# Linear attention's levels one slot later, the widest copied by ScalarE, other banks for its outputs, and own regions for the last feed-forward's inputs

## The chip, the cores and the metric

One core of a Trainium2 chip runs the whole program. The metric is the device time of one execution in microseconds; of the kernel before there are three runs. Four engines compute: TensorE (PE; matmuls and, as PEld, its weight loads), VectorE (DVE), ScalarE (ACT) and GpSimd (POOL). SyncE (SP) issues the weight transfers. They run side by side and wait for each other through semaphores.

## The reference, cut to what matters

```python
# h: [512 tokens, 1024 features], float32; three mixer layers, four feed-forwards
h = h + 0.5 * swiglu_ffn(rmsnorm(h))                   # ffn0
h = h + mixer1(rmsnorm(h)) @ w_mix_out                 # short convolution and gated delta rule
h = rmsnorm(h + 0.5 * swiglu_ffn(rmsnorm(h)))          # ffn1
# second block, layer 0: gated linear attention, 4 heads, beside attention on a memory of 256 rows
q, k, v, g, lr, mq = split(rmsnorm(h) @ gla_w_in)
b = cumsum(log_sigmoid(lr @ w_gate_up + b_gate) / 16)
A[i, j] = sum_d q[i, d] * k[j, d] * exp(b[i, d] - b[j, d])      # for i >= j
o = rmsnorm(A @ v) * silu(g)
h = h + concat(o, mem_attention(mq, mem)) @ w_out[0]
h = h + conv_ffn(rmsnorm(h))                           # ffn2
# layer 1: sparse attention (compressed, selected, windowed), beside memory attention
h = h + concat(nsa(rmsnorm(h)), mem_attention(mq, mem)) @ w_out[1]     # nsa_out
h = h + conv_ffn(rmsnorm(h))                           # ffn3
out = rmsnorm(h)
```

## The kernel before, in words

**Stages.** The program is a chain of dense stages, each a list of weight panels (128 x up to 1024) and output tiles (`Dense`, `Plan`). For a float32 result each operand is the sum of a high and a low part: ScalarE rounds the panel to `wH` (L407), VectorE subtracts to get `wL` (L445), and TensorE makes three matmuls, `wH`·`xH`, `wH`·`xL`, `wL`·`xH` (L589 to L591; with tokens as rows L583 to L585). There are four panel slots in `raw` and two in `wH`, `wL`: a panel is split one ahead of its use, once the panel two before it is used up. The order of work on each engine is written out by hand at the end of the program, one list for each engine: `after` on TensorE, `extra` and `ahead` on VectorE and `extra` on ScalarE hang other work behind or ahead of one tile of a dense stage.

**Linear attention.** `A` is not formed through one decay, but block by block in levels. The level of width w takes late queries and early keys of each block of 2w, both scaled by exponentials of gate sums relative to the block's middle. For a level, VectorE makes two differences of the gate sums (`level_sub_dve`, L2171, L2172), ScalarE their exponential (L2196), VectorE the products with queries and keys (`level_mul_dve`, L2214, L2215), TensorE the block products into banks 4 to 7 (`level_pe`), and VectorE copies them to `A256`, `A128` and `AD` (`take_dve`: L2232 for width 256, L2237 for 128, L2241 for 64, L2252 for narrower ones). There are widths 256 to 1, levels 0 to 8, and the diagonal blocks, level 9, which come first (L2290, copied at L2262). On TensorE the diagonal level runs ahead of stage gla_v, the wide one (level 0, L2300) behind its tile 1, the next ones behind tiles 3, 5, 7, 9 and 11 and behind tiles 0, 1 and 3 of gla_g. gla_v has 12 tiles of 256 columns in banks 0 to 3 in turn, copied by ScalarE (L1931); gla_g has 6 of 512, copied by VectorE in two pieces (L789, `evac_packed`). The memory attention's result stays in banks 2 and 3 until VectorE has made `m_lo` of it (L2063); tile 2 of gla_v waits for that. Then come eight outputs (`go_pe`: L2389, L2391, L2394), in banks 0 to 3 in turn, each copied by VectorE (L2417), squared by ScalarE (L2367) and summed by TensorE (L2401, `go_norm_pe`, from the fourth output on).

**The last feed-forward.** nsa_out writes 8 tiles, in two rounds of a loop of four, with `xH`, `xL` as inputs. VectorE adds each to `hT` (L827). ffn3_up reads `xH`, `xL` again, now filled from `hT`: ScalarE writes `xH` (`x_hi`, L845) once all matmuls of nsa_out are done (`refill_act`), VectorE `xL` (`x_lo`, L850), ScalarE squares (L860) for the norm, which GpSimd adds up (L907). ffn3_up's first tile takes the inputs one by one as they come. `g_hi`, `g_lo` hold the feed-forward's inner values for the second matmul.

```python
def bank_free_pe(pe, n, g):
    if n == 0 and g < 2:
        pe.wait_ge(sem("a_out"), g + 1)
...
def go_pe(pe, t):
    if t == 0:
        pe.wait_ge(sem("a_out"), a_before(len(LEVEL_ORDER)))
        wait_all(pe, stage_end("gla_g") + stage_end("gla_v"))
...
    o = bank[t % 4][0:96]
```

Of the kernel before, what the change touches and what calls it, by code (L numbers as in the profile page):

```python
# [5 lines left out]
ALU = mybir.AluOpType  # L6
# [128 lines left out]
def build(nc, A, out):  # L135

    with ExitStack() as ctx:
# [35 lines left out]
        g_hi_f = g_hi[:].bitcast(F32)  # L173
        w_hi3 = nc.alloc_sbuf_tensor_at("w_hi3", [P, SLOT], F32R, offset=at_arena + 4 * 10 * R)
# [30 lines left out]

        def up_stage(k, w, f):

            return Dense(f"ffn{k}_up", NF // 2, [[panel(w, KD, c + P * u, P, 2 * P)] for c in (0, FF) for u in range(2)],
                         [features(b, b, P, 0) for b in range(4)], (xH, xL), xfill(f))

        def down_stage(k, w):
# [4 lines left out]
            return Dense(f"ffn{k}_down", 1, panels, tiles, (g_hi, g_lo), None, by_rows=True)  # L216
# [478 lines left out]
        def g_split_act(act, k, f):  # L695
# [66 lines left out]
        def down_pe(pe, k):  # L762

            s = plan.stages[f"ffn{k}_down"]
            for f in range(NF):
# [3 lines left out]
                gh, gl = g_hi[:, f % 4, :], g_lo[:, f % 4, :]  # L769
# [1372 lines left out]
        A_COUNT = [2, NH, 2] + [1] * 7  # L2142

# [81 lines left out]
        def take_dve(dve, pos):  # L2225
# [3 lines left out]
            if n == 0:  # L2229
                for h in range(NH):  # L2230
                    dve.wait_ge(sem("a_sum"), base + h + 1)
                    nc.vector.tensor_copy(A256[:, h], bank[4 + h][:].rearrange("p (k s) -> p k s", k=2))\  # L2232
                      .then_inc(sem("a_out"), 1)
            elif n == 1:
# [30 lines left out]

        def bank_free_pe(pe, n, g):
# [1126 lines left out]
```

## Time and profile before

| | |
|---|---|
| median of 3 runs | 2419.6 us (2419.26 to 2421.55) |
| profiled execution | 2420.1 us, its span 2417.7 us |
| TensorE busy | 2360.8 us, 98% |
| VectorE busy | 1333.9 us, 55% |
| ScalarE busy | 921.3 us, 38% |
| GpSimd busy | 156.1 us, 6% |
| mean granted TensorE clock | 0.99 |
| linear attention, gla_v's first matmul to the first output | 1150.3 to 1251.5 us |
| ffn3_up's first matmul | 2040.0 us |

### The profile page before, as it was taken

The page shows a single profiled execution, that of the slowest core. Times are in us where ns is not written, and L with a number is a line of the kernel's source. Part 1 is how long each engine was busy: PE and PEld are TensorE (multiplying, and loading weights), DVE is VectorE, ACT ScalarE, POOL GpSimd, SP SyncE. Part 2 cuts the span into 40 slices and gives each one's busy share as a digit, 9 for nine tenths or more (in the row PEclk, how much of TensorE's full clock was granted, in tenths as well). Part 3 has the DMA queues.
Part 4 walks back from the last instruction along what each step waited for, and adds up shares of the span by engine and source line. Part 5 has one row for each costly group of instructions (what it writes and reads, how often), then busy time and mean ns, then how long its engine had stood idle before and what let it go on. Part 6 is the DMA issues. An engine that isn't in the chain of part 4 may idle for free.

```text
span 2417.7 us, 31976 instructions
## 1 busy us (share of the span) xinstructions
PE 2360.8 (98%) x12187; PEld 1927.1 (80%) x12187; DVE 1333.9 (55%) x2039; ACT 921.3 (38%) x1440; POOL 156.1 (6%) x151
## 2 busy tenths in 40 slices
PE   8999999999999999999999999999999989999999
PEld 7888887678778888877877888888887667888887
DVE  4444337667454444346867766644436874666633
ACT  4222225633442223244434333423224873433323
POOL 3000001024020000030001000000010001000001
PEclk9999999999999999999999999999999999999999
DMA  5333223220233332232213333232843102333322
GB/s 152 91 99 96 97 88 86 71 70 19 70 88 94 96 95 95 98 97 62 68 47 96 88 97 101 87 97 86 187 135 107 47 17 86 97 96 95 96 96 78
DMA packets 319650, 215.80 MB, mean 89 GB/s; under 512 B 49306, under 2 KB 302765, under 8 KB 319545
## 3 DMA queue, kind: packets, MB, share of 16 engines
q1 hardware_dynamic: 316280, 200.40, 28.8%
q0 software_dynamic: 3264, 13.94, 1.8%
q8 instruction: 73, 1.20, 0.2%
q14 instruction: 33, 0.26, 0.0%
HBM read 212.17 MB, written 8.44 MB: 91 GB/s over the span
## 4 chain that ended last, share of the span: by engine, by line
PE 88%; DVE 8%; ACT 2%; issue 1%; DMA 0%; POOL 0%; SPq 0%; POOLq 0%; DVEq 0%; ACTq 0%
PE bank L589 18%; PE bank L591 17%; PE bank L590 17%; PE bank L776 6%; PE bank L778 6%; PE bank L777 6%; PE bank L966 2%; DVE arena L2867 1%; PE bank L2815 1%; DVE wL L445 1%; DVE arena L2906 1%; PE bank L1716 1%; DVE xL L850 1%; PE bank L583 1%; PE bank L1822 1%
## 5 line engine op out<-in xcount | busy, mean ns | idle before, releaser
L589 PE MATMUL bank<-xH,wH 128*128 128x512 f32 x1920 | 761.8, 397 | 7.2 <-DVE xL L850 5.2
L591 PE MATMUL bank<-xH,wL 128*128 128x512 f32 x1920 | 750.8, 391 | 0.0
L590 PE MATMUL bank<-xL,wH 128*128 128x512 f32 x1920 | 750.6, 391 | 0.0
L445 DVE TENSOR_TENSOR wL<-raw,wH 128x1024 fp32r<-128x1024 f32 (+1 forms) x357 | 445.5, 1248 | 516.5 <-ACT wH L407 516.1
L407 ACT ACTIVATE wH<-raw 128x1024 fp32r<-128x1024 f32 (+1 forms) x357 | 374.9, 1050 | 758.4 <-PE bank L591 355.5
L589 PEld LDWEIGHTS bank<-xH,wH 128*128 128x128 f32 x1920 | 361.2, 188 | 95.5 <-issue 20.2
L590 PEld LDWEIGHTS bank<-xL,wH 128*128 128x128 f32 x1920 | 361.1, 188 | 79.1 <-issue 3.9
L591 PEld LDWEIGHTS bank<-xH,wL 128*128 128x128 f32 x1920 | 360.9, 188 | 78.3 <-issue 0.8
L776 PE MATMUL bank<-g_hi,wH 128*128 128x512 f32 x704 | 274.2, 390 | 1.5 <-DVE wL L445 1.5
L777 PE MATMUL bank<-g_lo,wH 128*128 128x512 f32 x704 | 273.9, 389 | 0.0
L778 PE MATMUL bank<-g_hi,wL 128*128 128x512 f32 x704 | 273.9, 389 | 0.0
L2481 ACT ACTIVATE arena<-arena,par 128x512 f32<-128x512 f32 x88 | 63.5, 723 | 271.9 <-DVE arena L2513 271.9
L776 PEld LDWEIGHTS bank<-g_hi,wH 128*128 128x128 f32 x704 | 132.2, 188 | 29.9 <-DVE wL L445 2.8
L778 PEld LDWEIGHTS bank<-g_hi,wL 128*128 128x128 f32 x704 | 132.2, 188 | 27.6
L777 PEld LDWEIGHTS bank<-g_lo,wH 128*128 128x128 f32 x704 | 132.2, 188 | 27.4
L2513 DVE TENSOR_TENSOR arena<-bank,rstd 128x512 f32<-128x512 f32 x88 | 60.6, 690 | 82.2 <-PE bank L591 82.1
L803 ACT ACTIVATE arena<-arena 128x512 f32<-128x512 f32 x44 | 27.6, 631 | 176.8 <-DVE arena L810 176.8
L907 POOL TENSOR_TENSOR rstd<-sq 128x512 f32<-128x512 f32 x7 | 9.7, 1384 | 1264.7 <-ACT sq L860 1264.7
L966 PEld LDWEIGHTS bank<-ident,arena 128*128 128x128 f32 (+4 forms) x467 | 54.5, 147 | 45.6 <-issue 23.1
L966 PE MATMUL bank<-ident,arena 128*128 128x128 f32 (+4 forms) x467 | 71.7, 295 | 18.6 <-DVE arena L2906 8.8
L812 DVE TENSOR_TENSOR arena<-bank,rstd 128x512 f32 (+1 forms) x44 | 30.4, 691 | 107.4 <-PE bank L591 107.4
L810 DVE TENSOR_TENSOR arena<-bank,rstd 128x512 f32<-128x512 f32 x44 | 30.2, 691 | 82.1 <-PE bank L591 82.0
(347 smaller groups left out, 2601.8 us busy)
## 6 DMA issues: line engine op xcount, KB each, us to landing
raw<-in_ffn_w_in SPq DMA_DIRECT2D x88, 512.0 KB, 3.8
raw<-in_w_up SPq DMA_DIRECT2D x88, 512.0 KB, 3.8
raw<-in_ffn_w_out SPq DMA_DIRECT2D x44, 512.0 KB, 3.5
raw<-in_w_down SPq DMA_DIRECT2D x44, 512.0 KB, 3.5
raw<-in_w_mix_in SPq DMA_DIRECT2D x28, 512.0 KB, 3.9
raw<-in_w_kv_shared SPq DMA_DIRECT2D x12, 512.0 KB, 6.3
rel_wide<-rel_rows POOLq DMA_DIRECT2D x12, 512.0 KB, 11.6
arena<-rel_wide POOLq DMA_DIRECT2D x12, 448.0 KB, 4.2
```

What stands on the lines that cost most here:

```text
L407: nc.scalar.activation(hi[:, 0:n], raw[:, k, 0:n], ACT.Copy).then_inc(sem("w_hi"), 1)
L445: nc.vector.tensor_tensor(lo[:, 0:n], raw[:, k, 0:n], hi[:, 0:n].bitcast(F32), ALU.subtract)\
L589: pe.matmul(o, wh, xa, start=a, stop=False)
L590: pe.matmul(o, wh, xb, start=False, stop=False)
L591: last = pe.matmul(o, wl, xa, start=False, stop=z)
L776: pe.matmul(bank[m][:], wh, gh, start=f == 0, stop=False)
L777: pe.matmul(bank[m][:], wh, gl, start=False, stop=False)
L778: last = pe.matmul(bank[m][:], wl, gh, start=False, stop=f == NF - 1)
L812: nc.vector.tensor_tensor(g[:, bass.ds(2 * i + t - 2, 1), :], one(bank[t][:]), one(rstd[:]), ALU.mult)\
L966: return pe.transpose(o, i, ident[0:k, 0:k])
L2481: nc.scalar.activation(cv[:, t, :], us[:, t, :], ACT.Copy, scale=conv_columns(s, i, t)[2])\
L2513: nc.vector.tensor_tensor(us[:, t, :], bank[t][:], rstd[:], ALU.mult).then_inc(sem("evac_dve"), 1)
```

## The change

- Levels: the diagonal level moves on TensorE from ahead of gla_v to behind its tile 1, levels 0 to 4 from behind tiles 1, 3, 5, 7, 9 to behind 3, 5, 7, 9, 11, level 5 from behind tile 11 to behind tile 0 of gla_g, levels 6 and 7 from behind tiles 0 and 1 to behind 1 and 2. Level 8 stays behind tile 3.
- VectorE's and ScalarE's lists are reordered to suit. The second pair of scans (`gate_scan_dve`) stands behind a split instead of ahead of it, `m_lo` ahead of the diagonal copies.
- Level 0's four banks are copied by ScalarE (`far_act`), with a semaphore of their own; `taken` counts the others.
- Output t goes to bank (t + 2) mod 4 and, for the first four, waits for that bank's own copy of gla_g instead of for all.
- nsa_out becomes one round of eight tiles. ffn3_up's inputs get regions of their own (`xH4`, `xL4`), so that `x_hi`, `square` and `x_lo` of tile j - 1 stand beside tile j of nsa_out. ffn3_down's inner values take the freed `xH`, `xL`.
- One activation of one column at the start is dropped.

```diff
+        xH4 = nc.alloc_sbuf_tensor_at("xH4", [P, KD, S], F32R, offset=at_arena + 4 * 10 * R)
+        xL4 = nc.alloc_sbuf_tensor_at("xL4", [P, KD, S], F32R, offset=at_arena + 4 * 12 * R)
...
+        def x_home(f):
+
+            return (xH4, xL4, xH4f) if f == 10 else (xH, xL, xHf)
+
+        def g_home(k):
+
+            return (xH[:, 0:4], xL[:, 0:4], xHf[:, 0:4]) if k == 3 else (g_hi, g_lo, g_hi_f)
...
-            return Dense(name, 2, [[panel(w, KD, P * j, P, 4 * P)] for j in range(4)],
-                         [features(b, b, P, 0) for b in range(4)], (xH, xL), xfill(f))
+            return Dense(name, 1, [[panel(w, KD, P * j, P)] for j in range(KD)],
+                         [features(j % 4, j, P, 0) for j in range(KD)], (xH, xL), xfill(f))
...
-                        pe.wait_ge(sem("go"), 5 + m)
+                        pe.wait_ge(sem("go"), 5 + (m + 2) % 4)
...
-            nc.scalar.activation(gain4[:, 0:1], eps[:], ACT.Copy).then_inc(sem("warm"), 1)
...
+        TAKEN = [2, 0, 2] + [1] * 7
...
+        def far_act(act):
+
+            for h in range(NH):
+                act.wait_ge(sem("a_sum"), a_before(1) + h + 1)
+                nc.scalar.activation(A256[:, h], bank[4 + h][:].rearrange("p (k s) -> p k s", k=2), ACT.Copy)\
+                  .then_inc(sem("far_out"), 1)
...
             elif n == 1:
-                pe.wait_ge(sem("a_out"), a_before(1) + g + 1)
+                pe.wait_ge(sem("far_out"), g + 1)
             elif n in (2, 3):
-                pe.wait_ge(sem("a_out"), a_before(1) + n + 1)
+                pe.wait_ge(sem("far_out"), n + 1)
...
             if t == 0:
-                pe.wait_ge(sem("a_out"), a_before(len(LEVEL_ORDER)))
-                wait_all(pe, stage_end("gla_g") + stage_end("gla_v"))
-            if t >= 4:
+                pe.wait_ge(sem("far_out"), NH)
+                pe.wait_ge(sem("a_out"), taken(len(LEVEL_ORDER)))
+                wait_all(pe, stage_end("gla_v"))
+            if t < 4:
+                pe.wait_ge(sem("evac_dve"), plan.evac(plan.stages["gla_g"], 0, t + 2))
+            else:
                 pe.wait_ge(sem("go"), t - 3)
...
-            dense_act(act, "nsa_out", nothing)
-            refill_act(act, 10, 7, "nsa_out", "ffn3_up")
+            ready = h_from("nsa_out")
+
+            def next_operand(k):
+                x_hi(act, 10, k, ready(k))
+                square(act, 7, k, ready(k))
+            dense_act(act, "nsa_out", nothing, extra={(0, j): lambda j=j: next_operand(j - 1) for j in range(1, KD)})
+            x_hi(act, 10, KD - 1, ready(KD - 1))
+            split_second(act, "ffn3_up")
+            square(act, 7, KD - 1, ready(KD - 1))
...
-            dense_dve(dve, "nsa_out", residual(1.0))
-            for k in range(KD):
-                x_lo(dve, 10, k)
+            dense_dve(dve, "nsa_out", residual(1.0), ahead={(0, j): lambda j=j: x_lo(dve, 10, j - 1) for j in range(1, KD)})
+            x_lo(dve, 10, KD - 1)
...
-            level_pe(pe, 0)
             dense_pe(pe, "gla_v", after={0: lambda: mem_round_pe(pe, 0, 5),
-                                         1: lambda: (level_pe(pe, 1), pe.wait_ge(sem("x_ready"), xbase(5) + 2)),
-                                         **{2 * n + 1: lambda n=n: level_pe(pe, n + 1) for n in range(1, 6)}})
-            dense_pe(pe, "gla_g", after={0: lambda: level_pe(pe, 7), 1: lambda: level_pe(pe, 8), 3: lambda: level_pe(pe, 9)})
+                                         1: lambda: (level_pe(pe, 0), pe.wait_ge(sem("x_ready"), xbase(5) + 2)),
+                                         **{2 * n + 3: lambda n=n: level_pe(pe, n + 1) for n in range(5)}})
+            dense_pe(pe, "gla_g", after={t: lambda t=t: level_pe(pe, t + 6) for t in range(4)})
```

What the reordering does to the queues is seen best in the instructions themselves. VectorE at the start of gla_v: `wL` is a split; L2119 are the scans; L2171, L2172 the differences, L2214, L2215 the products of a level; L2262 the diagonal copies, L2063 `m_lo`, L2232 the copies of the wide level. Before:

```order
L445 TENSOR_TENSOR wL<-raw,wH 128x1024
L2171 TENSOR_TENSOR arena<-arena 96x8x128
L2172 TENSOR_TENSOR arena<-arena 96x8x128
L2214 TENSOR_TENSOR arena<-arena 96x4x256
L2215 TENSOR_TENSOR arena<-arena 96x4x256
L2171 TENSOR_TENSOR arena<-arena 96x16x64
L2172 TENSOR_TENSOR arena<-arena 96x16x64
L2262 COPY_PREDICATED arena<-ident,bank 64x8x64 x4
L2063 TENSOR_TENSOR m_lo<-bank,m_hi 128x512 x2
L2214 TENSOR_TENSOR arena<-arena 96x8x128
L2215 TENSOR_TENSOR arena<-arena 96x8x128
L2232 COPY arena<-bank 128x512 x4
```

In the changed kernel the same operations have other line numbers (L456 the split, L2131 the scans, L2188, L2189 the differences, L2231, L2232 the products, L2075 `m_lo`, L2274 the diagonal copies):

```order
L456 TENSOR_TENSOR wL<-raw,wH 128x1024
L2131 SCALAR_TENSOR_TENSOR arena<-ones,arena 96x512 x2
L2188 TENSOR_TENSOR arena<-arena 96x8x128
L2189 TENSOR_TENSOR arena<-arena 96x8x128
L2231 TENSOR_TENSOR arena<-arena 96x4x256
L2232 TENSOR_TENSOR arena<-arena 96x4x256
L2075 TENSOR_TENSOR m_lo<-bank,m_hi 128x512 x2
L2188 TENSOR_TENSOR arena<-arena 96x16x64
L2189 TENSOR_TENSOR arena<-arena 96x16x64
L2274 COPY_PREDICATED arena<-ident,bank 64x8x64 x4
L2231 TENSOR_TENSOR arena<-arena 96x8x128
L2232 TENSOR_TENSOR arena<-arena 96x8x128
```

The split has moved ahead of the scans, `m_lo` ahead of a pair of differences and the diagonal copies, and the four copies of the wide level are gone. ScalarE in the same place, where L1931 copies a tile of gla_v, L407 is a split and L2196 an exponential. Before:

```order
L2196 ACTIVATE arena<-arena 96x2048
L2035 ACTIVATE m_hi<-bank 128x512 x2
L1931 ACTIVATE arena<-bank,rcol 128x256
L2196 ACTIVATE arena<-arena 96x2048
L1931 ACTIVATE arena<-bank,rcol 128x256 x2
L407 ACTIVATE wH<-raw 128x1024 x2
L1931 ACTIVATE arena<-bank,rcol 128x256
L2196 ACTIVATE arena<-arena 96x2048
```

Now (L2047 makes `m_hi`, L2213 is an exponential, L1943 a tile's copy, L418 a split, L2282 the wide level's copies):

```order
L2047 ACTIVATE m_hi<-bank 128x512 x2
L2213 ACTIVATE arena<-arena 96x2048
L1943 ACTIVATE arena<-bank,rcol 128x256
L2213 ACTIVATE arena<-arena 96x2048
L1943 ACTIVATE arena<-bank,rcol 128x256 x2
L418 ACTIVATE wH<-raw 128x1024 x2
L1943 ACTIVATE arena<-bank,rcol 128x256
L2282 ACTIVATE arena<-bank 128x512 x4
```

The memory result's copy stands ahead of the first exponential, and the wide level's copies follow the copy of tile 3.

## Rows read from the trace of the kernel before

**Rows 1.** The page: the span, TensorE's busy time, and ScalarE's split of a panel
```profile
span 2417.7 us, 31976 instructions
...
PE 2360.8 (98%) x12187; PEld 1927.1 (80%) x12187; DVE 1333.9 (55%) x2039; ACT 921.3 (38%) x1440; POOL 156.1 (6%) x151
...
L407 ACT ACTIVATE wH<-raw 128x1024 fp32r<-128x1024 f32 (+1 forms) x357 | 374.9, 1050 | 758.4 <-PE bank L591 355.5
```

**Rows 2.** Who TensorE waited for, 1100 to 1300: us in total, times, longest
```profile
PE bank L2323 <- DVE arena L2215: 3.0, 2, 2.7
PE bank L2300 <- DVE arena L2262: 3.0, 2, 2.7
```

**Rows 3.** Stretches: length, busy PE, PEld, DVE, ACT, POOL, granted clock, DMA
```profile
1160.27:1166.20 5.93, 5.62 (x18) 4.36 (x19) 5.88 (x8) 0.66 (x2) 0.00 (x0) 0.71 0.00 1
1220.80:1228.00 7.20, 7.20 (x74) 6.42 (x75) 6.26 (x7) 0.00 (x0) 0.00 (x0) 0.56 0.28 96
1251.50:1256.00 4.50, 4.50 (x34) 4.08 (x35) 0.69 (x1) 4.47 (x4) 0.00 (x0) 1.00 0.01 4
2039.95:2043.50 3.55, 3.54 (x10) 2.83 (x11) 3.55 (x6) 3.55 (x6) 0.00 (x0) 0.59 0.00 0
1749.00:1992.00 243.00, 224.82 (x1866) 167.82 (x1866) 155.13 (x562) 139.02 (x394) 13.15 (x25) 0.96 0.27 78
```

**Rows 4.** Timeline, TensorE, 1148 to 1252: start, us, instruction, idle before
```profile
1148.27 2.08 PE L2290 MATMUL bank<-arena 96*64 96x64 f32 x64
1160.27 1.10 PE L2300 MATMUL bank<-arena 96*128 96x256 f32 x4 [2.72 <-DVE arena L2262]
...
1186.46 2.06 PE L2323 MATMUL bank<-arena 96*64 96x32 f32 x64
1194.84 2.06 PE L2323 MATMUL bank<-arena 96*64 96x32 f32 x64 [0.38 <-DVE arena L2215]
1210.42 2.06 PE L2323 MATMUL bank<-arena 96*64 96x32 f32 x64
1220.80 3.63 PE L2323 MATMUL bank<-arena 96*64 96x32 f32 x64 [2.66 <-DVE arena L2215]
1251.46 1.08 PE L2389 MATMUL bank<-arena 128*96 128x128 f32 x8 [1.53 <-issue]
```

**Rows 5.** Timeline, VectorE, 1148 to 1237
```profile
1148.24 2.34 DVE L2119 TENSOR_TENSOR_SCAN arena<-ones,arena 96x512 f32<-96x512 f32 x2
1151.61 1.22 DVE L2171 TENSOR_TENSOR arena<-arena 96x1024 f32<-96x1024 f32 x1
...
1158.66 2.97 DVE L2262 COPY_PREDICATED arena<-ident,bank 64x512 f32<-64x512 uint32 x4
1161.65 1.29 DVE L2063 TENSOR_TENSOR m_lo<-bank,m_hi 128x512 fp32r<-128x512 f32 x2
...
1165.13 2.47 DVE L2232 COPY arena<-bank 128x512 f32<-128x512 f32 x4
1171.72 1.23 DVE L445 TENSOR_TENSOR wL<-raw,wH 128x1024 fp32r<-128x1024 f32 x1 [4.12 <-ACT wH L407]
...
1236.88 1.40 DVE L789 TENSOR_TENSOR arena<-bank,arena 96x512 f32<-96x512 f32 x2 [2.79 <-PE bank L591]
```

**Rows 6.** Timeline, ScalarE, 1147 to 1170
```profile
1147.58 1.07 ACT L2028 ACTIVATE arena<-bank 128x512 f32<-128x512 f32 x2
...
1169.12 0.47 ACT L1931 ACTIVATE arena<-bank,rcol 128x256 f32<-128x256 f32 x1 [8.20 <-PE bank L585]
```

**Rows 7.** Timeline, all engines, around the end of nsa_out
```profile
2034.17 1.28 POOL L907 TENSOR_TENSOR rstd<-sq 128x512 f32<-128x512 f32 x1 [96.18 <-ACT sq L860]
...
2037.36 5.01 ACT L845 ACTIVATE xH<-hT,par 128x512 fp32r<-128x512 f32 x8 [0.66 <-PE bank L591]
...
2038.12 6.33 DVE L850 SCALAR_TENSOR_TENSOR xL<-hT,par,xH 128x512 fp32r<-128x512 f32 x8
2039.95 0.76 PE L589 MATMUL bank<-xH,wH 128*128 128x512 f32 x1 [2.63 <-DVE xL L850]
```

More of the change, by code:

```diff
@@ L204, in features @@
                     "terms": [(j, nk, q * cols + at, width, x0 + q) for q in range(k)]}
+        def x_home(f):
+            return (xH4, xL4, xH4f) if f == 10 else (xH, xL, xHf)
+        def g_home(k):
+            return (xH[:, 0:4], xL[:, 0:4], xHf[:, 0:4]) if k == 3 else (g_hi, g_lo, g_hi_f)
         def up_stage(k, w, f):
             return Dense(f"ffn{k}_up", NF // 2, [[panel(w, KD, c + P * u, P, 2 * P)] for c in (0, FF) for u in range(2)],
-                         [features(b, b, P, 0) for b in range(4)], (xH, xL), xfill(f))
+                         [features(b, b, P, 0) for b in range(4)], x_home(f)[0:2], xfill(f))
         def down_stage(k, w):
@@ L215, in down_stage @@
                       "terms": [(f, P, m * P, P, f) for f in range(NF)]} for m in range(KD)]
-            return Dense(f"ffn{k}_down", 1, panels, tiles, (g_hi, g_lo), None, by_rows=True)
+            return Dense(f"ffn{k}_down", 1, panels, tiles, g_home(k)[0:2], None, by_rows=True)
         def ffn(k, w_in, w_out, f):
@@ L768, in down_pe @@
                 h = half_slot(s, 0, f)
-                gh, gl = g_hi[:, f % 4, :], g_lo[:, f % 4, :]
+                gh, gl = (x[:, f % 4, :] for x in g_home(k)[0:2])
                 for m in range(KD):
@@ L844, in x_hi @@
             act.wait_ge(*ready)
-            nc.scalar.activation(xH[:, k, :], hT[:, k, :], ACT.Copy, scale=gain(f, k)).then_inc(sem("x_hi"), 1)
+            nc.scalar.activation(x_home(f)[0][:, k, :], hT[:, k, :], ACT.Copy, scale=gain(f, k)).then_inc(sem("x_hi"), 1)
         def x_lo(dve, f, k):
             dve.wait_ge(sem("x_hi"), xbase(f) + k + 1)
-            nc.vector.scalar_tensor_tensor(out=xL[:, k, :], in0=hT[:, k, :], scalar=gain(f, k), in1=xHf[:, k, :],
+            _, lo, hi = x_home(f)
+            nc.vector.scalar_tensor_tensor(out=lo[:, k, :], in0=hT[:, k, :], scalar=gain(f, k), in1=hi[:, k, :],
                                            op0=ALU.mult, op1=ALU.subtract).then_inc(sem("x_ready"), 1)
@@ L2158, in a_before, with taken @@
             return sum(A_COUNT[:pos])
+        def taken(pos):
+            return sum(TAKEN[:pos])
         def level_sub_dve(dve, n):
@@ L2228, in take_dve @@
             base = a_before(pos)
[L2229 to L2234, printed above, removed]
+            if n == 1:
                 for g in range(2):
@@ L2245, in take_dve @@
                 dve.wait_ge(sem("a_sum"), base + 1)
-                dve.wait_ge(sem("a_out"), base)
+                dve.wait_ge(sem("a_out"), taken(pos))
                 w = WIDTHS[n]
@@ L2352, in values_act @@
                     take_value_act(act, 4 * j + 3)
+                if j == 0:
+                    far_act(act)
         def gg_act(act, half):
@@ L2376, in go_roots_act, with go_bank @@
                 inverse_root(act, 16 + h, gn[:, h, :])
+        def go_bank(t):
+            return bank[(t + 2) % 4]
         def go_pe(pe, t):
@@ L2416, in go_out_dve @@
                 dve.wait_ge(sem("go_sum"), t + 1)
-                nc.vector.tensor_copy(go[0:96, t, :], bank[t % 4][0:96, :]).then_inc(sem("go"), 1)
+                nc.vector.tensor_copy(go[0:96, t, :], go_bank(t)[0:96, :]).then_inc(sem("go"), 1)
                 if t:
@@ L3289, in _ @@
             dense_dve(dve, "gla_g", evac_packed(gg, rstd2),
[L3290 to L3294 removed]
+                      extra={(0, 0): lambda: (level_sub_dve(dve, 8), take_dve(dve, 6)), (0, 1): lambda: take_dve(dve, 7)},
+                      ahead={(0, 0): lambda: (level_sub_dve(dve, 7), take_dve(dve, 5), level_mul_dve(dve, 6)),
+                             (0, 1): lambda: level_mul_dve(dve, 7), (0, 3): lambda: (level_mul_dve(dve, 8), take_dve(dve, 8)),
+                             (0, 4): lambda: take_dve(dve, 9)})
             go_out_dve(dve)
```

34 lines of the change are left out of this document (13 added, 21 removed).

## The prediction, made before the changed kernel ran

> **What bounds the kernel now.** The page's busy times come first: TensorE is busy for 2360.8 of 2417.7 us [rows 1]. The reader is to see the difference, 56.9 us. An edit that takes nothing off TensorE's own work, and this one takes off none, can at best win part of that. The second view is TensorE's waits, in the two places that the diff touches. In the linear attention stage they are 3.0 and 3.0 us [rows 2] and 1.53 us [rows 4]; at the start of the last feed-forward it is 2.63 us [rows 7]. Third, the granted clock by stretches: after three of these waits it is below 1 while TensorE works, so each wait costs more than its length [rows 3]. Fourth, the timelines of TensorE, VectorE and ScalarE around the waits, which say what is late [rows 4 to 7]. I call the level of width 256 "wide", and v0 to v11 and g0 to g5 the tiles of the stages gla_v and gla_g.
>
> **What the waits are for.** At 1160.27 the wide level stands 2.72 us, then 0.30 [rows 2, 4]: its banks hold the diagonal blocks, which VectorE copies at 1158.66, behind two scans and six operations of 96x1024 [rows 5]. At 1194.84 and 1220.80 a level waits 0.38 and 2.66 us for products of VectorE [rows 4]. At 1251.46 the first output matmul waits 1.53 us, since it needs every copy of gla_g [rows 4]. At 2039.95 the feed-forward waits 2.63 us: the last residual, the first xH and the first xL come one after another from 2037.36 on, because xH is still being read until then [rows 7]. Idle in all: 3.02 + 0.38 + 2.66 + 1.53 + 2.63 = 10.22 us.
>
> **The clock behind them.** 5.93 us at a mean of 0.71, 7.20 at 0.56 and 3.55 at 0.59 [rows 3] lose 1.72 + 3.17 + 1.46 = 6.35 us against full clock. The stretch behind the 1.53 us wait has 1.00 and loses nothing [rows 3]. I take the three losses as consequences of the three waits of 2.6 us and more, because all three lie directly behind them, and one of them (at 2039.95) is behind dense 512-column work with no narrow matmul near. The Trainium skill, TensorE: Matmul & The Clock Gate, HAM oscillation, warns of idle gaps longer than any of these as what slows the array; by that rule these gaps would be harmless, the low clock would come from elsewhere, and the sum would be the idle alone, 10.2 us. The rows above show the clock lower behind gaps of 2.6 to 2.7 us, so the rows decide.
>
> **The change, part by part.** Removed on TensorE: nothing; the same matmuls in another order.
>
> (a) *Levels one slot later.* The diagonal level (2.08 us [rows 4]) goes from before v0 to behind v1, the wide one from behind v1 to behind v3. Start at 1148.3, when the diagonal level began. v0 takes 3.1 us, the 16 memory matmuls 1.0, v1 3.05, the diagonal level 2.0: 1157.5. Then TensorE needs m_lo. VectorE: the split for v0's second half now stands ahead of the scans, at 1148.2 to 1149.4, just in time for its use at about 1149.8. Then the scans (2.27) to 1151.7, four operations of 1.17 (six took 7.05, from 1151.61 to 1158.66 [rows 5]) to 1156.4, m_lo 1.29 to 1157.7. So TensorE waits some 0.2 us here: a new, small wait. v2 and v3 (2.95 each) end at 1163.6. VectorE meanwhile: two differences, then the diagonal copies, 2.97 us [rows 5], done at 1162.95. The wide level finds its banks free by 0.65 us, and without low clock takes 3.5 us. v4 starts at 1167.1 and needs one more split: ScalarE's half at 1162.7 to 1163.7 (behind v3's first half), VectorE's behind a product pair, at 1166.45. Slack 0.65 us. The 3.02 us wait goes, with its 1.72 of clock.
>
> (b) *ScalarE copies the wide level.* VectorE loses four copies, 2.47 us [rows 5]. ScalarE gains four of 128x512 from a bank; two such take 1.07 [rows 6], so 2.1 us, at 1165.3 to 1167.7. It stood 8.20 us idle ahead of 1169.12 [rows 6], which is the cover; without that cover they would delay v0 to v3's evacuations, which v4 to v7 need. TensorE needs these banks again at the next level, at about 1173: slack over 5 us.
>
> (c) *The later levels.* A level and two v tiles take 8.0 us (1186.46 to 1194.46, the wait left out), a level and a g tile 7.7 (1210.42 to 1218.14) [rows 4]. Levels 3 to 8 in count now have that much more time for their products, and the tight places are elsewhere. The split that v8 waits for depends on v7's first half, as before, and arrives about 0.2 us ahead. The last level keeps its slot behind g3: from g2's end TensorE has g3 and one level, 7.5 us; VectorE has g2's copies 1.40, a split 1.23 and the last product pair 2.4 [rows 5], done after 5.0. Slack 2.5 us. So the waits of 0.38 and 2.66 go, with 3.17 of clock. New waits: none of which I could make more than 0.2 us.
>
> (d) *Other banks for the outputs.* The first four outputs take banks 2, 3, 0, 1, in the order in which gla_g's copies free them, and wait for one tile's copy each. Bank 2's is 19 us old by then. g5's copy (1.40 us) is wanted three outputs, 6.5 us, later. The 1.53 goes. ScalarE's first square comes 6 us behind the first output now; it is wanted 7 to 8.7 us behind it. Slack at least 1 us.
>
> (e) *Own regions for the last feed-forward's inputs.* xH and xL of tiles 0 to 6 are made during nsa_out, tile 7's 1.5 to 2.3 us after its end, while TensorE's first 21 matmuls take 4.8. The 2.63 goes, with its 1.46. ScalarE's 8 operations (5.01 us) and VectorE's 8 (6.33) [rows 7] move under matmuls: per tile of 5.44 us (24 matmuls) ScalarE has a split of 1.05 [rows 1], xH 0.63 and a square of about that, 2.3 in all; VectorE has a split 1.23, xL 0.79 and the residual, under 3.
>
> (f) *The dropped first activation* is 0.2 us on an idle ScalarE: worth nothing.
>
> **Sum.** 10.22 + 6.35 - 0.2 = 16.4 us. The profiled execution took 2420.1 in all, 2.4 beyond its span; it lies 0.5 above the median of 2419.6. 2420.1 - 16.4 = 2403.7, from the median 2403.2: I say 2403.5.
>
> **Bounds.** Unknown is what the clock does elsewhere. The 243 us of the sparse attention have a mean clock of 0.96 [rows 3], 9.7 us lost in several short falls; everything there now comes 12 us earlier, and no row says how many falls remain. One fall as behind 1160.27 is 1.7 us, so I allow two more or two fewer: +-3.4 us, taken as 0. The new 0.2 us wait behind 2 us of narrow matmuls may bring one too: 0 to 1.7, taken as 0, because 0.38 us behind such matmuls brought none: the next fall came only at 1220.80 [rows 3, 4].
>
> **Rivals.**
> - *The clock falls at the levels with or without the wait.* The two falls in the linear attention begin beside matmuls of 96 rows, which stay. For it: there is a fall there each time; against it: the levels at 1186.46 to 1210.42 have none, and 2039.95 has one without them. Then 1.72 + 3.17 stay: 2408.4. The Trainium skill, TensorE: Matmul & The Clock Gate, A second HAM failure mode, describes this direction: brief pauses between groups of matmuls, with banks taking turns, are enough to make the clock swing. The 1.53 us wait with clock 1.00 behind it speaks against it [rows 3, 4].
> - *VectorE slips at one place.* The slacks of 0.2 and 0.65 us (m_lo, the banks of the wide level, the splits of v4 and v8) are small against my errors. A wait under half a microsecond costs only itself; one that grows to the size of that at 1220.80 brings 2.66 + 3.17: 2409.3. Against it: VectorE is relieved of 2.47 us at this point.
> - *The change does not do what it says in the last part*: ScalarE's squares wait for GpSimd's sums, its queue fills behind them, and xH comes no earlier. Then 4.1 us stay: 2407.6. Against it: a sum takes 1.28 us [rows 7] of a 5.44 us tile.
> - *Slower.* VectorE's queue is strict; if its extra order (copies after the pair that they free) puts it behind TensorE by more than the slack at every level from 3 to 8, each of six levels waits and pays the clock, at 4.4 (2.7 + 1.7) each: 26 against 16.4, so 2430. It decides itself once VectorE is more than some 5 us late at v4 and never catches up. Against it: its own idle time of 4.12 us there [rows 5] and of 2.79 at g3.
> - *No change*: the time won returns as waits of the same size further on, for weights perhaps. No wait of the splits on a transfer stands among those I read.
>
> **How the numbers follow.** Forecast 0.60; clock stays 0.15; VectorE slips once 0.13; last part fails 0.06; no change 0.03; slower 0.03. The forecast's own range is 2403.5 - 3.4 to 2403.5 + 3.4 + 1.7, 2400 to 2408.6; the next two cases and the third lie at 2407.6 to 2409.3, so 2400 to 2410 leaves out less than 2 in 10. 0.2% is 4.8 us, about what a measurement of this kernel can tell from no change: faster is below 2414.8, which holds in all but the last two cases.
>
> **What would show it.** Right: TensorE's busy time falls by about 6, its idle time by about 10; no wait of the wide level for the diagonal copies; no wait ahead of the output matmuls; the feed-forward's first matmul directly behind nsa_out's last; clock 1.00 in both stages. The output matmuls begin some 12 us earlier. Wrong: a wait for a split or for m_lo of over 0.5 us, a clock under 1 between the levels, or a wait on the new copies of ScalarE.

## The result, and the profile after

| | before | changed |
|---|---|---|
| median of 4 runs each | 2420.57 us (2419.26 to 2423.28) | 2404.68 us (2400.78 to 2405.53) |
| profiled execution, span | 2420.1, 2417.7 us | 2404.13, 2402.0 us |
| TensorE busy | 2360.8 us | 2356.9 us |
| TensorE idle | 56.9 us | 45.1 us |

The changed kernel is faster: ratio 0.9925, 95% interval 0.9912 to 0.9939, some 16 us. Line numbers have moved by 11 to 25. The first lines of the page, which answer to [rows 1]:

```profile
span 2402.0 us, 31966 instructions
...
PE 2356.9 (98%) x12187; PEld 1923.3 (80%) x12187; DVE 1330.7 (55%) x2035; ACT 923.1 (38%) x1443; POOL 160.1 (7%) x151
```

The same 12187 matmuls, and 3.9 us less of busy time. Most of that is clock: TensorE is busy for 46.5 us at half clock before and for 40.1 now, a loss of 23.2 us against 20.0, so 3.2 of the 3.9. TensorE's idle time fell by 11.8 us. Who TensorE waits for from 1100 to 1300 (us in total, times, longest), against [rows 2]:

```profile
PE bank L594 <- DVE m_lo L2075: 0.2, 1, 0.2
```

One wait is left, the new one for `m_lo`. From 1990 to 2060 the same view has no row at all; there stood the 2.63 us of [rows 7]. TensorE's timeline, against [rows 4]: L2309 is the diagonal level, L2319 the wide one, L2342 those of width 32 and less, L2414 the outputs.

```profile
1157.19 2.08 PE L2309 MATMUL bank<-arena 96*64 96x64 f32 x64
1159.48 0.38 PE L594 MATMUL bank<-wH,xH 128*128 128x256 f32 x1 [0.20 <-DVE m_lo L2075]
1165.33 3.62 PE L2319 MATMUL bank<-arena 96*128 96x256 f32 x16
...
1197.21 2.06 PE L2342 MATMUL bank<-arena 96*64 96x32 f32 x64
1204.86 2.06 PE L2342 MATMUL bank<-arena 96*64 96x32 f32 x64
...
1220.17 2.06 PE L2342 MATMUL bank<-arena 96*64 96x32 f32 x64
1227.82 2.06 PE L2342 MATMUL bank<-arena 96*64 96x32 f32 x64
1240.83 1.03 PE L2414 MATMUL bank<-arena 128*96 128x128 f32 x8
```

The brackets, which show idle time, are gone but for the 0.20: every level comes directly behind its tile, the wide one takes 3.62 us instead of 1.10 + 0.30 + 4.54, and the last ones have an even beat of 7.65 us. The granted clock of stretches (length, busy PE, PEld, DVE, ACT, POOL, clock), against [rows 3]:

```profile
1159.48:1175.00 15.52, 15.52 (x117) 15.10 (x118) 15.40 (x15) 9.71 (x13) 0.00 (x0) 1.00 0.30 69
1197.00:1230.00 33.00, 33.00 (x420) 27.71 (x419) 30.72 (x32) 10.43 (x10) 0.00 (x0) 1.00 0.29 81
1240.00:1246.00 6.00, 6.00 (x45) 5.40 (x44) 2.69 (x4) 3.52 (x3) 0.00 (x0) 1.00 0.19 57
2026.00:2032.00 6.00, 6.00 (x28) 4.99 (x27) 2.67 (x3) 2.19 (x3) 1.81 (x1) 1.00 0.17 50
1100.00:1116.00 16.00, 16.00 (x46) 9.65 (x44) 5.66 (x8) 2.97 (x2) 0.00 (x0) 0.68 0.24 59
1749.00:1992.00 243.00, 224.84 (x1816) 166.59 (x1815) 157.35 (x562) 143.55 (x400) 13.15 (x25) 0.96 0.26 78
```

Clock 1.00 in all four places where waits were removed; the third of them, the outputs, had 1.00 before too [rows 3]. The fifth row is a place the change does not touch, and it got slower. In the kernel before the stretch has 0.89:

```profile
1100.00:1115.00 15.00, 15.00 (x57) 10.10 (x57) 6.00 (x9) 3.25 (x3) 0.00 (x0) 0.89 0.28 70
```

It costs 16 x 0.32 = 5.1 us now and 15 x 0.11 = 1.7 before. The sparse attention, last row, is unchanged at 0.96. VectorE around the wide level, against [rows 5]:

```profile
1158.13 1.29 DVE L2075 TENSOR_TENSOR m_lo<-bank,m_hi 128x512 fp32r<-128x512 f32 x2
...
1161.61 3.06 DVE L2274 COPY_PREDICATED arena<-ident,bank 64x512 f32<-64x512 uint32 x4
...
1166.97 2.35 DVE L456 TENSOR_TENSOR wL<-raw,wH 128x1024 fp32r<-128x1024 f32 x2
```

The diagonal copies end at 1164.67, 0.66 ahead of the wide level at 1165.33. ScalarE's new copies, against [rows 6], are 1.81 us for three and 0.60 for the fourth. Nothing waits for them, and ScalarE stands idle for 2.28 us before its next copy of a tile, at 1171.86:

```profile
1166.91 1.81 ACT L2282 ACTIVATE arena<-bank 128x512 f32<-128x512 f32 x3
1168.98 0.60 ACT L2282 ACTIVATE arena<-bank 128x512 f32<-128x512 f32 x1 [0.27 <-PE bank L2319]
```

nsa_out's last matmul begins at 2026.14 and ffn3_up's first at 2026.37, with no wait between them. Against [rows 7], only tile 7's operations are left then, the residual, `xH`, `xL` and the square, beside running matmuls; VectorE's two are:

```profile
2026.57 0.69 DVE L839 SCALAR_TENSOR_TENSOR hT<-bank,hT 128x512 f32<-128x512 f32 x1 [2.40 <-PE bank L602]
2028.05 0.75 DVE L863 SCALAR_TENSOR_TENSOR xL<-hT,par,xH 128x512 fp32r<-128x512 f32 x1 [0.79 <-ACT xH L857]
```

### The profile page after: what moved, and what is told of

Its sections match the earlier page's. It is cut to its first block, busy times and chain, and to the rows that moved or that the text cites. A ratio compares the mean times of both kernels' runs of the same rounds, so it can differ in the third digit from the quotient of the medians.

```text
span 2402.0 us, 31966 instructions
## 1 busy us (share of the span) xinstructions
PE 2356.9 (98%) x12187; PEld 1923.3 (80%) x12187; DVE 1330.7 (55%) x2035; ACT 923.1 (38%) x1443; POOL 160.1 (7%) x151
## 4 chain that ended last, share of the span: by engine, by line
PE 89%; DVE 8%; ACT 1%; issue 1%; DMA 0%; POOL 0%; SPq 0%; POOLq 0%; DVEq 0%; ACTq 0%
PE bank L600 18%; PE bank L602 18%; PE bank L601 18%; PE bank L788 6%; PE bank L790 6%; PE bank L789 6%; PE bank L979 2%; DVE arena L2892 1%; PE bank L2840 1%; DVE xL L863 1%; DVE wL L456 1%; DVE arena L2931 1%; PE bank L1728 1%; PE bank L594 1%; PE bank L595 1%
## 5 line engine op out<-in xcount | busy, mean ns | idle before, releaser
L456 DVE TENSOR_TENSOR wL<-raw,wH 128x1024 fp32r<-128x1024 f32 (+1 forms) x357 | 444.7, 1246 | 511.8 <-ACT wH L418 511.3
L418 ACT ACTIVATE wH<-raw 128x1024 fp32r<-128x1024 f32 (+1 forms) x357 | 374.9, 1050 | 753.2 <-PE bank L602 347.7
L788 PE MATMUL bank<-g_hi,wH 128*128 128x512 f32 x528 | 205.6, 389 | 0.7 <-DVE wL L456 0.7
L789 PE MATMUL bank<-g_lo,wH 128*128 128x512 f32 x528 | 205.4, 389 | 0.0
L790 PE MATMUL bank<-g_hi,wL 128*128 128x512 f32 x528 | 205.4, 389 | 0.0
L788 PEld LDWEIGHTS bank<-g_hi,wH 128*128 128x128 f32 x528 | 99.1, 188 | 22.1 <-DVE wL L456 1.5
L789 PEld LDWEIGHTS bank<-g_lo,wH 128*128 128x128 f32 x528 | 99.1, 188 | 20.5
L790 PEld LDWEIGHTS bank<-g_hi,wL 128*128 128x128 f32 x528 | 99.1, 188 | 20.5
L979 PEld LDWEIGHTS bank<-ident,arena 128*128 128x128 f32 (+4 forms) x467 | 54.5, 147 | 45.5 <-issue 23.2
```

Source lines behind the costliest of these rows:

```text
L418: nc.scalar.activation(hi[:, 0:n], raw[:, k, 0:n], ACT.Copy).then_inc(sem("w_hi"), 1)
L456: nc.vector.tensor_tensor(lo[:, 0:n], raw[:, k, 0:n], hi[:, 0:n].bitcast(F32), ALU.subtract)\
L788: pe.matmul(bank[m][:], wh, gh, start=f == 0, stop=False)
L789: pe.matmul(bank[m][:], wh, gl, start=False, stop=False)
L790: last = pe.matmul(bank[m][:], wl, gh, start=False, stop=f == NF - 1)
L979: return pe.transpose(o, i, ident[0:k, 0:k])
```

## The experiments

Ratios are against the kernel before on the same chip, with the 95% interval. Single runs of one kernel spread over several us (the kernel before from 2414 to 2429 in three batches), so an effect of 2 to 4 us is read in the profile, and the medians only bear it out or not. The experiments ran in three batches, each on a chip of its own. The first (the regions, the banks and the wide level's copies undone, the waits filled) had no run of the change itself beside it, so there only the ratios can be compared with the change's 0.9925 to 0.9934.

**The change as it is, again (two batches).**

> The changed kernel as it is, for a comparison on the same chip with the other runs of this set. Theory: its time differs from run to run by a few us, as many as 2 to 5, because stretches of low clock outside the edited places come and go (in its first profile the low clock behind the gate's narrow matmuls, near 1104, lasted 10.2 us where the kernel before had 3.4). So: 0.993 of the kernel before, and a spread of some 5 us between its runs.

> The change as it is, for comparison on this chip: 2404.6, between 2402 and 2407, with a low clock of 3.4 to 10.2 us at the gate's matmuls and none at the levels nor at the last feed-forward.

Medians 2404.48 (2402.92 to 2406.63), ratio 0.9929 (0.9917 to 0.9941), and 2405.44 (2402.80 to 2407.16), ratio 0.9934 (0.9919 to 0.9948). In the profile of the second the span is 2400.7, TensorE is busy for 2353.6 us, and the gate's stretch has 0.89. In that of the first the sparse attention has 0.94, where it had 0.96:

```profile
1100.00:1116.00 16.00, 16.00 (x63) 10.82 (x62) 8.66 (x14) 6.84 (x9) 0.00 (x0) 0.89 0.17 41
```

```profile
1749.00:1992.00 243.00, 225.30 (x1765) 165.56 (x1765) 157.63 (x562) 143.58 (x400) 13.14 (x25) 0.94 0.27 78
```

So the loss at the gate changes with the same program, 1.8 us here and 5.1 in the profile above, and that of the attention too, 14.6 us against 9.7. At the levels and at ffn3_up the clock was 1.00 in each.

**The regions undone: part (e).**

```diff
-            return (xH4, xL4, xH4f) if f == 10 else (xH, xL, xHf)
+            return (xH, xL, xHf)
```

and nsa_out and the operands behind it as before.

> The changed kernel with the last feed-forward's own regions taken back (nsa_out in two rounds, xH and xL filled when its matmuls are done). Theory: the wait of 2.63 us ahead of ffn3_up and the low clock behind it, 1.46 us by the rows of before, come back, so 4.1 us more than the changed kernel, some 2408 to 2409. Rival (the clock's falls are not tied to that wait): 2.6 us more, with a granted clock of 1.00 behind the wait. Rival (the part won nothing, since GpSimd's sums hold ScalarE up): the same time as the changed kernel.

Median 2409.55 (2405.39 to 2411.79), ratio 0.9938 (0.9923 to 0.9954). Timeline of TensorE, and the stretch behind it:

```profile
2029.24 0.76 PE L600 MATMUL bank<-xH,wH 128*128 128x512 f32 x1 [2.62 <-DVE xL L863]
```

```profile
2028.30:2032.00 3.70, 2.76 (x7) 2.21 (x8) 3.70 (x6) 3.70 (x7) 0.25 (x1) 0.56 0.00 0
```

The wait is back at its old length with a low clock behind it: 2.62 + 3.70 x 0.44 = 4.2 us, as expected. The span is 5.1 us above that of the change. The ratio lies 0.0004 to 0.0013 (1 to 3 us) above the change's three and its interval overlaps theirs, so the price rests on the profile.

**The regions alone, in the kernel before.** Part (e) as in the diff of the change, nothing else.

> The kernel before with the own regions for the last feed-forward's inputs alone (nsa_out in one round, xH4 and xL4). Theory: its wait of 2.63 us and the low clock behind it, 1.46, vanish: 4.1 us less than the kernel before, no other stretch changed. Rival (the clock's part is not tied to the wait): 2.6 us less.

Median 2419.03 (2413.60 to 2423.36), ratio 0.9987 (0.9974 to 0.9999): 3 us where 4.1 were expected, at the edge of what can be told. The wait of the feed-forward is gone. The levels keep their waits, with more low clock than in [rows 3]:

```profile
1163.90:1170.80 6.90, 6.21 (x15) 5.00 (x16) 6.82 (x10) 1.35 (x2) 0.00 (x0) 0.51 0.00 1
1225.40:1232.40 7.00, 6.41 (x71) 5.78 (x72) 6.81 (x8) 0.02 (x1) 0.00 (x0) 0.51 0.30 104
```

The wide level's wait costs 6.90 x 0.49 = 3.4 us of clock here, against 1.72 in the profiled execution of before.

**The banks undone: part (d).**

```diff
-            return bank[(t + 2) % 4]
+            return bank[t % 4]
```

and the first output waits for all of gla_g again.

> The changed kernel with the outputs in banks 0 to 3 in turn again, the first of them waiting for all of gla_g's copies. Theory: the wait of 1.53 us comes back without low clock, so 1.5 us more than the changed kernel, which is less than a set of runs may tell, and a wait ahead of the first output matmul in the profile. Rival (a wait of 1.5 us can bring a fall of the clock too): 3.2 us more, with a granted clock under 1 behind it.

Median 2408.85 (2404.66 to 2411.50), ratio 0.9937 (0.9921 to 0.9953). The wait ahead of the outputs, and the clock around it:

```profile
PE bank L2412 <- DVE arena L801: 1.7, 1, 1.7
```

```profile
1239.00:1250.00 11.00, 9.31 (x67) 8.09 (x66) 4.95 (x8) 6.03 (x6) 0.00 (x0) 1.00 0.05 13
```

The wait is back and costs its own 1.7 us, no clock. The ratio differs by only 0.0003 to 0.0012 from the change's three, so the times do not show the effect by themselves.

**The wide level copied by VectorE: part (b).**

```diff
-                act.wait_ge(sem("a_sum"), a_before(1) + h + 1)
-                nc.scalar.activation(A256[:, h], bank[4 + h][:].rearrange("p (k s) -> p k s", k=2), ACT.Copy)\
+                dve.wait_ge(sem("a_sum"), a_before(1) + h + 1)
+                nc.vector.tensor_copy(A256[:, h], bank[4 + h][:].rearrange("p (k s) -> p k s", k=2))\
```

at the end of `first_levels`.

> The changed kernel with the widest level's four copies on VectorE again, behind the product pair that ends its first list, in the place where they stood before. Theory: VectorE waits there for the wide level's matmuls, so the split that tile 4 of gla_v needs comes some 3.5 us late; TensorE waits 2 to 3 us for it, and the clock falls behind that: 2 to 5 us more than the changed kernel. Rival (moving the copies to ScalarE was not needed, one slot later is all): no wait for that split, the same time as the changed kernel.

Median 2408.59 (2404.46 to 2410.75), ratio 0.9931 (0.9915 to 0.9947). TensorE's timeline and the clock behind it:

```profile
1169.00 0.36 PE L594 MATMUL bank<-wH,xH 128*128 128x256 f32 x1 [2.01 <-DVE wL L456]
```

```profile
1169.00:1175.00 6.00, 6.00 (x50) 6.00 (x51) 5.96 (x6) 2.27 (x2) 0.00 (x0) 1.00 0.78 178
```

And VectorE's copies:

```profile
1165.12 2.60 DVE L2283 COPY arena<-bank 128x512 f32<-128x512 f32 x4
```

The copies put VectorE late for v4's split, and TensorE waits 2.01 us: their 2.60 less the slack of 0.65 that was forecast makes 1.95. Two parts of the expectation failed: VectorE did not wait for the wide level's matmuls (no idle time stands ahead of its copies), and the clock behind the wait is 1.00. So ScalarE's copies are worth 2 us by the profile (the ratio, 0.9931, cannot be told from the change's), and only because the levels had moved: the next run shows that alone they do not take away the two large waits.

**The old slots: parts (a) and (c) undone, (b), (d), (e) kept.**

```diff
+            level_pe(pe, 0)
             dense_pe(pe, "gla_v", after={0: lambda: mem_round_pe(pe, 0, 5),
-                                         1: lambda: (level_pe(pe, 0), pe.wait_ge(sem("x_ready"), xbase(5) + 2)),
-                                         **{2 * n + 3: lambda n=n: level_pe(pe, n + 1) for n in range(5)}})
-            dense_pe(pe, "gla_g", after={t: lambda t=t: level_pe(pe, t + 6) for t in range(4)})
+                                         1: lambda: (level_pe(pe, 1), pe.wait_ge(sem("x_ready"), xbase(5) + 2)),
+                                         **{2 * n + 1: lambda n=n: level_pe(pe, n + 1) for n in range(1, 6)}})
+            dense_pe(pe, "gla_g", after={0: lambda: level_pe(pe, 7), 1: lambda: level_pe(pe, 8), 3: lambda: level_pe(pe, 9)})
```

VectorE's and ScalarE's lists follow the kernel before, `far_act` behind the copy of v1.

> Levels back in the slots of the kernel before on all three engines, ScalarE still copying the wide one, banks and regions as in the change. My theory: the slots are what removes the waits, since VectorE stood idle 4.12 us right behind its four copies and the relief ends there; so 3.0 us of wait come back at the wide level and 0.4 and 2.7 at the later ones, and with them about 4.9 us of clock: some 11 us slower than the change, about 2415.5. Rival one: ScalarE's copies alone suffice, no wait of the levels over 0.5 us: as the change, 2404.6. Rival two: only the wide level waits, 3.0 + 1.7: 2409.3.

Median 2419.47 (2410.06 to 2424.55), ratio 0.9978 (0.9963 to 0.9993), 14.0 us above the change on the same chip. Timeline and clock:

```profile
1165.16 6.90 PE L2319 MATMUL bank<-arena 96*128 96x256 f32 x16 [2.73 <-DVE arena L2274]
1226.65 3.63 PE L2342 MATMUL bank<-arena 96*64 96x32 f32 x64 [2.66 <-DVE arena L2232]
```

```profile
1164.80:1171.60 6.80, 6.44 (x15) 5.21 (x16) 5.22 (x7) 2.81 (x5) 0.00 (x0) 0.50 0.00 1
1226.00:1234.00 8.00, 7.35 (x75) 6.54 (x76) 6.91 (x8) 0.08 (x1) 0.00 (x0) 0.57 0.35 119
```

Both large waits are there, to within 0.01 us of [rows 4] and although VectorE has four copies less. Waits of 5.4 and clock of 6.80 x 0.50 + 8.00 x 0.43 = 6.8 make 12.2 of the 14.0 us. By the ratios, 0.9978 against 0.9934, the difference is 10.7 us, and the single runs go from 2410 to 2425, so the total is known to some us only. I had expected 11 with 4.9 of clock; the clock's part came out larger in this profile, as in the run with the regions alone. The slots carry most of the change.

**The waits filled, in the kernel before.** Matmuls that nothing reads stand where TensorE waited: 12 ahead of the wide level, 12 ahead of the late one, three of float32 behind nsa_out.

```diff
+            if n == 0:
+                for _ in range(FILL[0]):
+                    pe.matmul(bank[7][:], xH[:, 0, 0:P], xH[:, 1, :], start=True, stop=True)
```

> The kernel before, with matmuls that nothing reads in its three longest waits: 12 of 512 columns ahead of the wide level and ahead of level 7, and 3 float32 ones of 512 columns behind nsa_out. The waits are still there, but TensorE works in them. Theory (the waits bring the low clock): granted clock 1.00 in the three stretches that had 0.71, 0.56 and 0.59, the work behind them shorter by 1.7, 3.2 and 1.5 us, and a time up to 6.3 us below the kernel before; some of it lost where the filling overruns the wait. Rival (the narrow matmuls bring it): the clock still falls at the two levels, and at most 1.5 us is won.

Median 2418.83 (2414.67 to 2422.51), ratio 0.9982 (0.9971 to 0.9993). The filler, the level behind it, and the clock there and at the other two places:

```profile
1157.47 2.91 PE L2299 MATMUL bank<-xH 128*128 128x512 f32 x12
1160.42 1.10 PE L2309 MATMUL bank<-arena 96*128 96x256 f32 x4
```

```profile
1160.40:1166.40 6.00, 5.68 (x32) 4.93 (x33) 5.96 (x8) 0.63 (x2) 0.00 (x0) 1.00 0.01 1
1219.00:1226.00 7.00, 7.00 (x87) 5.84 (x86) 6.50 (x8) 0.00 (x0) 0.00 (x0) 1.00 0.30 108
2033.00:2040.00 7.00, 6.97 (x26) 4.48 (x25) 6.61 (x9) 6.68 (x11) 1.86 (x3) 1.00 0.09 26
```

The levels are where they were, with their 96 rows, and TensorE no longer stands still but for the 0.3 us behind the wide level's first four matmuls: clock 1.00 at all three. So the narrow matmuls alone do not bring the clock down there; it takes the wait. The waits are still spent, on fillers, so what is won is clock alone: 0.0018 of 2420, about 4 us (2 to 7 by the interval), where [rows 3] have 6.35. Its profile agrees: behind both levels, the same matmul of the sparse attention starts at 1786.25 instead of 1790.63, 4.4 us earlier, where the clock at the two levels had cost 4.89.

**The rest: `m_lo` behind the differences.** One wait made longer by hand.

```diff
-                mem_out_dve(dve, 0, xbase(5), m_lo, m_hi_f)
                 level_sub_dve(dve, 2)
+                mem_out_dve(dve, 0, xbase(5), m_lo, m_hi_f)
```

> The change with m_lo back behind one pair of differences: VectorE makes it 2.4 us later, so TensorE stands 0.2 + 2.4 = 2.6 us ahead of v2. My theory: a wait of that size brings the clock down behind it, about 1.7 us more, so 4.1 in all: 2408.7, with a granted clock near 0.7 or less in the stretch behind it. Rival: the clock is not moved by a wait here, as it was not by 1.7 and 2.0 us in other places: 2.4 us, 2407.0, clock 1.00 behind it. The later levels still come without a wait in both.

Median 2407.13 (2404.65 to 2410.97), ratio 0.9937 (0.9922 to 0.9951), 1.7 us above the change on the same chip. Its profile:

```profile
1160.17 0.39 PE L594 MATMUL bank<-wH,xH 128*128 128x256 f32 x1 [2.56 <-DVE m_lo L2075]
```

```profile
1161.40:1164.90 3.50, 3.50 (x19) 3.50 (x19) 3.42 (x5) 0.37 (x1) 0.00 (x0) 0.54 0.00 0
```

The profile has the wait and the low clock, 2.4 + 3.50 x 0.46 = 4.0 us; the medians show 1.7, less than the wait alone and nearer to the rival's 2.4 than to my 4.1. The profile is that of the slowest of the six runs (2410.97; the other five take 2404.65 to 2407.40). It shows that the fall can happen here; whether it does so in most executions stays open.

**The gate's matmuls spread.** On TensorE, heads 1 to 3 of the gate go between the matmuls of gla_q's tile 1 (ahead of its panels' terms 1, 3 and 5) instead of all four heads ahead of it.

```diff
-            for h in range(NH):
+            for h in heads:
...
+                     mid={(1, 2 * h - 1): lambda h=h: gate_pe(pe, (h,)) for h in (1, 2, 3)})
```

> The changed kernel with the four gate matmuls of 16 rows, one behind tile 0 of gla_q as before and three between tile 1's matmuls, after every second group of three, instead of four in a row. Theory (the low clock near 1104 comes from some 4.5 us in which TensorE works, but in few rows): it vanishes, and the 1.7 to 5 us that it cost are won. Rival (it comes from something else, or the spread costs as much, since VectorE and ScalarE get the gate's sums later and the memory scores wait for them): no gain, or a new wait in gla_q.

> The gate's narrow matmuls spread over tile 1 of gla_q again, now beside the unchanged change on the same chip. My theory: no low clock near 1104 in its profile, where the change has 3.4 to 10.2 us of it, so 1.7 to 5 us faster than the change: 2401.5. Rival: the fall only moves to another place, since the clock's falls come and go: no difference, 2404.6.

Medians 2402.86 (2400.03 to 2408.26), ratio 0.9927 (0.9913 to 0.9941), and 2404.15 (2402.90 to 2405.78), ratio 0.9925 (0.9911 to 0.9939). Both profiles have clock 1.00 from 1100 to 1116, the first:

```profile
1100.00:1116.00 16.00, 16.00 (x65) 9.44 (x64) 8.67 (x14) 6.47 (x8) 0.00 (x0) 1.00 0.19 50
```

The fall is gone and no wait came for it, in two profiles; each of the twelve profiles of this document with the four in a row has 0.68 to 0.89 in this stretch. The medians are 1.6 and 1.3 us below the change's on the same chips, the right side both times, and the intervals overlap almost wholly: a likely gain that these runs can't secure. If one wanted a version ahead of both, it is this one.

**A filler in the sparse attention.** There the clock is 0.96 for 243 us. One float32 matmul that nothing reads goes ahead of a turn, in the two widest parts: twelve in all.

```diff
+            if br == 0 and t is not None and t >= 2:
+                pe.wait_ge(sem("n_pts"), 2 * j - 1)
+                pe.matmul(bank[5][:], ident[:], hT[:, 0, :], start=True, stop=True)
```

> The changed kernel with one float32 matmul of 512 columns that nothing reads (0.87 us) ahead of the turns of the two widest parts in the sparse attention, where TensorE waits ten times for 0.9 us for VectorE's scaling. Theory: the filling hides in these waits; of the five stretches of low clock in the attention (1.7 us each) some vanish: 0 to 6 us won. Rival (TensorE is late where it does not wait; the filling delays the turns and so ScalarE's copies behind them): slower by up to 10 us (12 fillings of 0.87).

Median 2415.64 (2410.23 to 2419.74), ratio 0.9977 (0.9966 to 0.9987): 11 us slower than the change. In the changed kernel's profile TensorE waits there for VectorE ten times:

```profile
PE bank L979 <- DVE arena L2931: 8.8, 10, 1.1
```

With the fillers these ten waits are gone, a new one stands in their place, and the clock from 1749 to 1992 is 0.96 as in the change's profile:

```profile
PE bank L2811 <- ACT arena L2988: 7.2, 7, 2.3
```

The twelve fillers of 0.87 us, 10.4 in all, are about the 11 us that were lost: they won no clock and, with the new wait, next to no waiting. The rival came out. A filler pays only in time that stays idle anyway.

## Why the prediction was right

The forecast was 2403.5 us in a range of 2400 to 2410, faster; measured were 2404.68, 2404.48 and 2405.44. The total lies nearer than its terms: in the profiled execution it is 0.7 us off, because terms that nobody forecast cancel. The gate took 3.4 us more, a wait of 1.6 us far ahead of the change was missing, and small pieces took off another 1.1. So the mechanism is right, and that the miss is so small is partly luck. By its steps:

- **(a)** *Levels one slot later.* Right, to the new 0.2 us wait (0.20) and the slack of the wide level (0.65 forecast, 0.66 read). With the old slots the waits of 2.72 and 2.66 come back at 2.73 and 2.66.
- **(b)** *ScalarE copies.* Right: 2.4 us against 2.1, without a wait for them. Giving them back to VectorE costs one wait of 2.01.
- **(c)** Right: no wait and an even beat of 7.65 us (7.7 forecast).
- **(d)** and **(e)** Right, each shown by undoing it, in the profiles rather than in the times: 1.7 us, and 2.62 with 1.6 of clock.
- **(f)** was not tried alone.
- **The clock behind the waits** (6.35 us): for these three places the mechanism is right, the size was read from one execution and is small for others. Two other profiles with the levels' waits lose 6.8 us at them instead of 1.72 + 3.17.
- **TensorE's busy time** was to fall by about 6 and fell by 3.9. The term that failed is the bound "what the clock does elsewhere", taken as 0: the gate's stretch took 3.4 us more in this execution (5.1 against 1.7), at the edge of the bound of 3.4, which one repeat exceeds in the attention alone (14.6 against 9.7). 6.35 - 3.4 leaves 2.9; of the other 1.0, 0.3 is less low clock in the attention and at the very end, and 0.7 is busy time at the same clock in pieces under 0.4 us, unexplained.
- **TensorE's idle time** fell by 11.8 where the sum has 10.22 - 0.2 = 10.0. Of the other 1.8, 1.63 is a wait in an earlier stage that the change does not touch (the row below this list). In the profile of the changed kernel TensorE runs at a mean clock of 0.57 from 455 to 459, ahead of that place, and gets there too late to wait; in both repeats the wait is there again.
- **The outputs** were to begin some 12 us earlier and do by 10.6 (1240.83 against 1251.46): the gate takes 3.4 back, and the missing early wait gives 1.6.

```profile
461.46 1.91 PE L1616 MATMUL bank<-arena,ident 4*128 4x512 f32 x3 [1.63 <-ACT arena L1247]
```

**What the prediction left out.** It took the length of the wait as what tells a costly one from a harmless one, on the strength of three waits of 2.6 us and more with low clock behind them and one of 1.53 with none. The trace of the kernel before has shorter ones with low clock right behind them:

```profile
561.35 1.90 PE L1729 MATMUL bank<-arena 128*128 128x128 f32 x8 [2.07 <-DVE arena L1515]
1790.63 0.61 PE L589 MATMUL bank<-xH,wH 128*36 128x512 f32 x1 [1.97 <-DVE xL L850]
```

```profile
561.40:565.00 3.60, 3.60 (x17) 3.60 (x18) 3.24 (x6) 0.00 (x0) 3.60 (x4) 0.53 0.00 0
1790.60:1794.00 3.40, 3.37 (x9) 1.52 (x10) 3.40 (x6) 3.40 (x7) 3.06 (x6) 0.54 0.50 139
```

The wait of 1.63 us has 0.57 behind it, from 461.46 to 469.4. So waits of 1.63, 1.97 and 2.07 us had low clock behind them there, while 1.53, 1.7 and 2.01 us had 1.00 in linear attention. What else decides is not known. It did not hurt the forecast: each of its own waits came out as it was read.

The rivals: *the clock falls at the levels with or without the wait* fell by the filled waits and by every profile of the change. *VectorE slips at one place* happened in no profile of the change, though taking back one of two helps ((b), or the place of `m_lo`) makes it slip by 2.0 to 2.6 us: the slacks are as thin as they were worked out. *The last part does nothing*, *slower* and *no change* fell by the profile: no wait from 1990 to 2060, none of the levels, and 15.7 us less span. The Trainium skill, TensorE: Matmul & The Clock Gate, HAM oscillation, warns of longer idle gaps than any of these. Here waits of 2.56 to 2.73 us had a clock of 0.50 to 0.71 behind them in every profile that has one. So the measurement decides, and the sum by idle time alone (the forecast and 6.35 more, 2409.8) would have missed by 5.

## What to carry to other kernels

When TensorE is busy 98% of the time, list its waits and look at the clock behind each: the waits of 2.6 us cost 4 to 6 here. Do not judge by the wait's length alone: of those between 1.5 and 2.1 us some cost only themselves and some had low clock behind them, so read each one's stretch. Work that another engine makes for TensorE late is best given one more slot of independent matmuls; a lighter queue alone (ScalarE's copies) left both large waits, as VectorE's idle time swallowed the relief. Where single runs spread by more than the effect, undo one part and read whether its wait comes back; the medians of six runs did not separate 2 us.

## What the runs showed of the hardware that I had not expected

The clock also falls with TensorE busy throughout. The gate's four matmuls take 16 rows and 512 columns each (the trace has two records for each, so eight), and nothing idles before or in them. In the profiles of the changed kernel and of the second repeat:

```profile
1102.13 5.67 PE L2113 MATMUL bank<-arena,gate_up 16*96 16x512 f32 x8
```

```profile
1101.12 3.65 PE L2113 MATMUL bank<-arena,gate_up 16*96 16x512 f32 x8
```

The same eight took 5.67 us in one execution and 3.65 in the other. In the second they ran at clock 1.00 and the fall came directly behind them:

```profile
1101.12:1104.77 3.65, 3.65 (x11) 1.24 (x10) 2.99 (x5) 0.31 (x1) 0.00 (x0) 1.00 0.00 0
1104.80:1109.00 4.20, 4.20 (x12) 3.30 (x13) 1.88 (x2) 1.91 (x1) 0.00 (x0) 0.59 0.24 57
```

In both the matmuls of 128 rows behind them went on at low clock (0.68 and 0.89 over 16 us). With the four spread among matmuls of 128 rows the clock was 1.00 in both profiles. The levels' matmuls of 96 rows had 1.00 in every profile in which nothing waited ahead of them. So a wait is not the only thing that can stand ahead of a fall. Whether it is these matmuls' few rows or something else that the four in a row have in common, such as what runs just ahead of them, was not tried.
